# A mixture-of-experts layer whose down projection keeps tokens still and streams w_down

## What is computed

```
xf     = rmsnorm(x, g)                       # 1024 tokens x 1024
logits = xf @ w_router + b_router            # 32 experts
top_logits, top_idx = top_k(logits, 4)       # 4 experts a token
top_w  = softmax(top_logits)
for expert e, on the tokens that chose it:
    gu     = xb @ w_gate_up[e] + b_gate_up[e]          # 1024 -> 2048
    gate   = min(gu[:, 0::2], 7)
    up     = clip(gu[:, 1::2], -7, 7)
    hidden = (up + 1) * gate * sigmoid(1.702 * gate)   # 1024
    y      = hidden @ w_down[e] + b_down[e]            # 1024 -> 1024
x = x + sum over a token's experts of top_w * y
```

## Time and profile before

| | us |
|---|---|
| median of three executions | 2376.84 |
| profiled execution | 2372.35 |
| its span | 2370.5 |
| TensorE busy (matmul) | 2273.3 |
| VectorE busy | 941.1 |
| ScalarE busy | 460.3 |
| GpSimd busy | 225.1 |

### The profile page before, as it was taken

The page is one execution under the profiler, slowest core; times in us unless marked ns, Lnnn a source line. Parts: engine busy times, 40 slices in busy tenths (PEclk is TensorE's granted clock), DMA queues, the critical chain, the costliest instruction groups (busy, mean ns, idle before and its releaser), DMA issues.

```text
span 2370.5 us, 43566 instructions
## 1 busy us (share of the span) xinstructions
PE 2273.3 (96%) x17841; PEld 2164.4 (91%) x17842; DVE 941.1 (40%) x2192; ACT 460.3 (19%) x848; POOL 225.1 (9%) x172
## 2 busy tenths in 40 slices
PE   6999999999969999999999999999999999999997
PEld 5878888777869999999999999999999999999997
DVE  6434434875363333233333333433333332333332
ACT  4243143664101111111111111111111111111110
POOL 1101101100000100001010001100010110001001
PEclk9999999999979999999999999999999999999998
DMA  4222222105378887788888877886888886888882
GB/s 163 98 71 72 89 89 65 62 2 186 114 234 265 270 284 237 236 272 268 288 277 288 278 239 248 274 278 220 289 271 283 271 265 216 286 290 272 287 271 36
DMA packets 250615, 504.05 MB, mean 213 GB/s; under 512 B 7994, under 2 KB 36718, under 8 KB 250238
## 3 DMA queue, kind: packets, MB, share of 16 engines
q1 hardware_dynamic: 234268, 451.96, 54.9%
q0 software_dynamic: 14912, 45.71, 9.7%
q10 hardware_dynamic: 1344, 5.01, 0.7%
HBM read 469.46 MB, written 31.10 MB: 211 GB/s over the span
## 4 chain that ended last, share of the span: by engine, by line
PE 91%; DVE 4%; issue 3%; DMA 1%; ACT 0%; POOL 0%; DVEq 0%; ACTq 0%; SPq 0%; POOLq 0%
PE bank L1053 43%; PE bank L1064 19%; PE bank L804 12%; PE bank L1041 3%; DVE hx L1413 2%; PE bank L1012 2%; PE bank L921 2%; PE bank L908 2%; PE bank L956 1%; PE bank L958 1%; PE bank L957 1%; PE bank L1004 1%; PE bank L886 1%; PE bank L812 1%; PE bank L898 0%
## 5 line engine op out<-in xcount | busy, mean ns | idle before, releaser
L1053 PE MATMUL bank<-hx,ring 128*128 128x140 f32 (+1 forms) x8192 | 1037.6, 288 | 26.2 <-issue 16.7
L1053 PEld LDWEIGHTS bank<-hx,ring 128*128 128x128 f32 x8192 | 1021.4, 197 | 33.2 <-issue 32.2
L1064 PE MATMUL bank<-hx,ring 128*128 128x140 f32 (+1 forms) x4096 | 514.7, 287 | 0.0
L1064 PEld LDWEIGHTS bank<-hx,ring 128*128 128x128 f32 x4096 | 507.0, 190 | 0.0
L760 ACT ACTIVATE hx<-hx 128x168 f32<-128x168 f32 x256 | 87.9, 343 | 1447.0 <-DVE hx L1484 1447.0
L1484 DVE TENSOR_SCALAR hx<-bank,hx 128x168 f32<-128x168 f32 x256 | 100.4, 392 | 639.4 <-PE bank L1053 638.9
L1509 DVE TENSOR_SCALAR hx<-bank,hx 128x168 f32<-128x168 f32 x256 | 100.5, 392 | 353.8 <-PE bank L1064 353.8
L573 POOL DMA_INDIRECT out_x<-mix,hx x66 | 99.8, 1513 | 825.4 <-ACT mix L753 780.9
L552 POOL DMA_INDIRECT mix<-xn_scratch,hx x66 | 64.7, 981 | 718.8 <-DVE hx L1408 708.7
L804 PE MATMUL bank<-hx_r,mix_r 128*128 128x512 f32 x480 | 116.1, 401 | 7.9 <-DVE hx_r L1147 7.9
L804 PEld LDWEIGHTS bank<-hx_r,mix_r 128*128 128x128 f32 x480 | 92.1, 193 | 28.4 <-issue 9.2
(11 more groups left out here) (202 smaller groups left out, 1697.8 us busy)
## 6 DMA issues: line engine op xcount, KB each, us to landing
ring<-in_w_gate_up SPq DMA_DIRECT2D x128, 2048.0 KB, 10.8
ring<-in_w_down SPq DMA_DIRECT2D x64, 2048.0 KB, 8.8
mix<-in_w_in SPq DMA_DIRECT2D x14, 1024.0 KB, 5.0
work<-in_w_in SPq DMA_DIRECT2D x14, 1024.0 KB, 5.0
ring<-in_x SPq DMA_DIRECT2D x8, 512.0 KB, 8.2
hx<-in_w_out SPq DMA_DIRECT2D x1, 4096.0 KB, 14.1
work<-in_x ACTq DMA_DIRECT2D x8, 512.0 KB, 4.8
out_x<-work SPq DMA_DIRECT2D x8, 512.0 KB, 4.4
```

The source lines that it names most:

```text
L1053: mm = e.matmul(bank[f % 2][:, part * CAP:part * CAP + w], gu_ring[:, k, f * 256 + part:(f + 1) * 256:2], xT[:, k, 0:w], start=k == 0, sto ...
L1064: return e.matmul(bank[2 + j % 2][:, 0:w], dn_ring[:, k, j * P:(j + 1) * P], hid[:, k, 0:w], start=k == 0, stop=k == KD - 1)
```

## The change

The down projection is turned round. `hid` is now the stationary operand and w_down streams as moving operand, 512 columns a matmul, so that the result has tokens on partitions, and no transposes back are needed. As a stationary operand has at most 128 columns, one matmul series serves the first 128 tokens (`down_main`, banks 2 and 3, two halves t of the output by eight k). Tokens past 128 go in rounds r of 32 (`down_over`): the stationary operand is 32 tokens wide, and each quarter j of the output columns (256) goes to its own group of 32 array columns and PSUM partitions of bank 7. A round is done only where the block has more than 128 (or 160) tokens, by a branch on the count. CAP becomes 192, the widths 140, 168 and 192.

The bias b_down, which was added per partition, is now put into PSUM first, by bf16 matmuls with a stationary selector `sel` of the expert (a three-way split of b_down's float32 rows into bf16 sums; it is made once before the loop, on ScalarE and VectorE).

The token list has three columns of 128 slots: the first 128 tokens and, for each round, 32 tokens four times over, once for each output quarter. Gathers and adds are three indirect DMAs each: one of 128 rows of 4 KB and two of 128 quarter rows of 1 KB. `y_m` and `y_o`, which hold the scaled result, lie over the gathered rows `xg`, `xg_o`; ScalarE writes them at the end of the block itself (`weigh_rows`) after the next block's tokens have been turned, and GpSimd issues the next gather before the block's own adds. Token transposes are 8 + 4 of 128 x 128. w_down is loaded again only after the block's last down matmul (both halves wait for m_dn at n*2+2).

```diff
-CAP = 168
+OV = 32
+GR = P // OV
+RO = 2
+CAP = P + RO * OV
+NH = 1 + RO
-WIDTHS = (140, CAP)
+WIDTHS = (140, 168, CAP)
...
                 for c in range(2):
-                    e.wait_ge(m_dn, n * 8 + (4 * c - 4))
+                    e.wait_ge(m_dn, n * 2 + 2)
...
             def gather():
-                for h in range(2):
-                    e.indirect_dma_start(out=xg[:, h], out_offset=None, in_=xn_dram,
-                                         in_offset=bass.IndirectOffsetOnAxis(ap=idx[:, h:h + 1], axis=0)).then_inc(g_in, 16)
+                e.indirect_dma_start(out=xg, out_offset=None, in_=xn_dram,
+                                     in_offset=bass.IndirectOffsetOnAxis(ap=idx[:, 0:1], axis=0)).then_inc(g_in, 16)
+                for r in range(RO):
+                    e.indirect_dma_start(out=xg_o[:, r], out_offset=None, in_=xn_quarters,
+                                         in_offset=bass.IndirectOffsetOnAxis(ap=idx[:, 1 + r:2 + r], axis=0)).then_inc(g_in, 16)
...
             def block_dmas(n):
-                add_rows(n)
                 e.wait_ge(l_ok, n + 2)
-                e.wait_ge(g_tr, n * 3 + 3)
+                e.wait_ge(sc_done, n * 48 + 48)
                 e.sem_inc(pool_go, 1)
                 gather()
+                add_rows(n)
...
             def weigh_rows(n):
-                e.wait_ge(sc_done, n * 32 + 16)
-                for h in range(2):
-                    for q in range(2):
-                        m = 2 * h + q
-                        e.wait_ge(m_ytr, n * 4 + (m + 1))
-                        e.activation(yo[:, h, q * 512:(q + 1) * 512], bank[4 + m][0:HC, :], ACT.Copy,
-                                     scale=w_sc[:, h:h + 1]).then_inc(m_yo, 1)
+                e.wait_ge(l_keep, n + 1)
+                e.wait_ge(g_tr, n * 4 + 8)
+                for t in range(2):
+                    e.wait_ge(m_dn, n * 2 + (t + 3))
+                    e.activation(y_m[:, t * CH:(t + 1) * CH], bank[2 + t][:, :], ACT.Copy, scale=w_sc[:, 0:1]).then_inc(m_yo, 1)
+                for r in range(RO):
+                    e.activation(y_o[:, r], bank[7][:, r * 2 * P:(r + 1) * 2 * P], ACT.Copy,
+                                 scale=w_sc[:, 1 + r:2 + r]).then_inc(m_yo, 1)
...
             def turn_tokens():
-                for k in range(KD):
-                    for h in range(2):
-                        at = (k % 3) * CAP + h * HC
-                        mm = e.transpose(bank[4 + k // 3][:, at:at + HC], xg[:, h, k * P:(k + 1) * P],
-                                         cst[0:HC, C_ID:C_ID + HC])
-                    if k in (2, 5, 7):
-                        mm.then_inc(g_tr, 1)
+                for m in range(2):
+                    for q in range(4):
+                        mm = e.transpose(bank[4 + m][:, q * P:(q + 1) * P], xg[:, (4 * m + q) * P:(4 * m + q + 1) * P], ident)
+                    mm.then_inc(g_tr, 1)
+                for r in range(RO):
+                    for c in range(2):
+                        mm = e.transpose(bank[6][:, (2 * r + c) * P:(2 * r + c + 1) * P], xg_o[:, r, c * P:(c + 1) * P], ident)
+                    mm.then_inc(g_tr, 1)
...
+            def down_bias(t):
+                e.matmul(bank[2 + t][:, :], sel, bias_d[:, t * CH:(t + 1) * CH], start=True, stop=False,
+                         skip_group_check=True)
+            def over_bias():
+                for r in range(RO):
+                    for j in range(GR):
+                        e.matmul(bank[7][quarter_rows(j), r * 2 * P:(r + 1) * 2 * P], sel[:, 0:OV],
+                                 bias_d[:, j * 2 * P:(j + 1) * 2 * P], start=r == 0, stop=False, skip_group_check=True)
+            def down_main(n, t, k):
+                if t == 0:
+                    e.wait_ge(m_hid, n * 8 + (k + 3))
+                if k == 0:
+                    e.wait_ge(dn_in[t], n * 16 + 16)
+                mm = e.matmul(bank[2 + t][:, :], hid[:, k, 0:P], dn_ring[:, k, t * CH:(t + 1) * CH], start=False,
+                              stop=k == KD - 1, skip_group_check=True)
+                if k == KD - 1:
+                    mm.then_inc(m_dn, 1)
+            def down_over(r):
+                for k in range(KD):
+                    for j in range(GR):
+                        e.matmul(bank[7][quarter_rows(j), r * 2 * P:(r + 1) * 2 * P],
+                                 hid[:, k, P + r * OV:P + (r + 1) * OV], dn_ring[:, k, j * 2 * P:(j + 1) * 2 * P],
+                                 start=False, stop=k == KD - 1, skip_group_check=True)
...
                     mm.then_inc(m_gu, 1)
-                    if f == 0:
-                        turn_rows(n)
                     if f == 5:
...
+                e.wait_ge(s_sel, n + 1)
+                down_bias(0)
+                for k in range(KD):
+                    down_main(n, 0, k)
+                down_bias(1)
+                for k in range(4):
+                    down_main(n, 1, k)
+                e.wait_ge(g_in, n * 48 + 96)
+                turn_tokens()
+                for k in range(4, KD - 1):
+                    down_main(n, 1, k)
+                e.wait_ge(l_ok, n + 2)
+                over_bias()
+                with e.If(tokens > P):
+                    down_over(0)
+                if w > P + OV:
+                    with e.If(tokens > P + OV):
+                        down_over(1)
+                down_main(n, 1, KD - 1)
```

More of the change, by code:

```diff
@@ L62 @@
 GALPHA = 1.702
-C_ID, C_MB, C_BO, C_LS, C_ON, C_CA = (P * i for i in range(6))
+C_ID, C_ON, C_MB, C_BO, C_LS, C_CA = (P * i for i in range(6))
 C_IO = 6 * P
-C_I32 = C_IO + CAP
+C_I32 = C_IO + NH * P
 C_TID = C_I32 + NE
@@ L88, in constants @@
     t[:, C_CA:C_CA + P] = r <= c
-    t[:, C_IO:C_IO + CAP] = np.arange(CAP)
+    t[:, C_IO:C_IO + NH * P] = np.concatenate([np.arange(P)] + [P + OV * j + np.arange(P) % OV for j in range(RO)])
+    t[:, C_SEL:C_SEL + NE + 1] = r % NE == np.arange(NE + 1)[None, :]
+    t[:, C_J] = np.arange(P) // OV
     t[:, C_I32:C_I32 + NE] = np.arange(NE)
@@ L558, in _ @@
             e.wait_ge(e_st[1], 128)
-            e.dma_start(b_rows[:, 2048:3072], b_down[0]).then_inc(sc_done, 16)
+            for g in range(3):
+                e.dma_start(b_raw[g * NE:(g + 1) * NE], b_down[0]).then_inc(sc_done, 16)
             e.wait_ge(l_ok, 1)
@@ L769, in _ @@
                     block_act(n)
-            weigh_rows(more + NE)
         @block.tensor
@@ L1001, in token_list @@
             def token_list():
-                for h in range(2):
+                for h in range(NH):
                     for i in range(NT):
-                        mm = e.matmul(bank[7][0:HC, 5 * h:5 * h + 5], hot[:, i, h * HC:(h + 1) * HC], tw_s[:, i, :],
+                        mm = e.matmul(bank[7][:, 5 * h:5 * h + 5], hot[:, i, h * P:(h + 1) * P], tw_s[:, i, :],
                                       start=i == 0, stop=i == NT - 1)
@@ L1020, in _ @@
             e.wait_ge(bias_in, 16)
-            e.wait_ge(sc_done, 16)
             e.wait_ge(e_x2, 16)
-            for j in range(24):
-                if j < 16:
-                    src = b_rows[:, (j % 8) * 256 + j // 8:(j % 8) * 256 + 256:2]
-                else:
-                    src = b_rows[:, 2048 + (j - 16) * P:2048 + (j - 15) * P]
-                mm = e.transpose(bank[j // 12][:, (j % 12) * NE:(j % 12 + 1) * NE], src, cst[0:NE, C_ID:C_ID + NE])
+            for j in range(16):
+                mm = e.transpose(bank[j // 8][:, (j % 8) * NE:(j % 8 + 1) * NE],
+                                 b_rows[:, (j % 8) * 256 + j // 8:(j % 8) * 256 + 256:2], cst[0:NE, C_ID:C_ID + NE])
@@ L1047, in block_matmuls @@
+            def block_matmuls(n, w, tokens):
+                e.wait_ge(g_xT, n * 4 + 4)
                 for f in range(KD):
@@ L1113, in _ @@
                     block_pe(n)
-            turn_rows(more + NE)
         @block.vector
@@ L1444, in _ @@
             e.wait_ge(bias_ok, 3)
-            for m in range(3):
-                e.wait_ge(g_tr, m + 1)
+            for g in range(1, 3):
+                e.wait_ge(b_cast, g)
+                rows = slice(0, 3 * NE) if g == 1 else slice(2 * NE, 3 * NE)
+                e.tensor_tensor(b_raw[rows], b_raw[rows], bias_d[rows], ALU.subtract).then_inc(b_sub, 1)
+            for m in range(4):
+                e.wait_ge(g_tr, m + 1 if m < 2 else 4)
                 tokens_out(m)
-            for s_ in (m_up, m_gs, m_hid):
+            for s_ in (m_up, m_gs, m_hid, m_dn):
                 e.sem_inc(s_, 2)
+            e.sem_inc(m_yo, 4)
             grid = [P, NX, NE]
@@ L1505, in block_dve @@
                         list_out(n + 1)
-                e.wait_ge(m_ytr, n * 4 + 4)
-                for j in range(KD):
-                    e.wait_ge(m_dn, n * 8 + (j + 1))
-                    e.tensor_scalar(yT[:, j, :], bank[2 + j % 2][:, 0:CAP], be[:, 16 + j:17 + j], None, ALU.add)\
-                        .then_inc(m_y, 1)
-                    if j == 6:
```

(6 more changed lines are left out.)

204 lines of the change are left out of this document (96 added, 108 removed).

## The result

Slower. Four executions after the change took 2391.02 to 2396.31 us, median 2393.39, against 2375.59 (2370.44 to 2377.72) of the kernel before on the same chip: ratio 1.0081, 95% interval 1.0064 to 1.0098. The forecast was 2365, faster. That 2393 lies inside the stated range of 2350 to 2432 is luck: the range reached so far up mostly for rivals 1 and 3, slow column groups and late gathers, and neither came. The profiled execution spans 2390.0 us against 2370.5, at a mean granted clock of 0.973 against 0.981.

The account below looks back on a forecast made before the run. The loop was taken as a TensorE sum of streamed columns. Loop -19, fetch +4, gathers +2, before the loop +4.5, end -3 gave -11.5 us: about 2365 against the median 2376.84, range 2350 to 2432.

Parts of the forecast that it names:

- rival 1: Extra-token rounds: only two column groups run at a time, +65 us, 2430 (singly 2560); chance 0.20.
- Rival 3: Token gathers come late, so TensorE stands 1.5 us a block before the token transposes: +46 us, 2411; chance 0.13.
- Instruction fetch: Expert loop: longer code makes wide blocks jump further; +4 us taken, bounds -10 to +15.
- Rival 4: Expert loop: two fetch stalls in every wide block and one in some others, +25 us, 2390; chance 0.07.
- all that a block gains together: Each block's new down matmuls, bias, token list, token transposes and shape changes: 17.0 us, times 32 blocks 544.
- A round: Pass over 32 extra tokens, all four column groups at once: 3.65 us, 19 passes 69 us, bounds 69 to 265.
- rival 2: Extra-token rounds: four column groups run at a third of the time, not a quarter; +17 us, 2382; chance 0.10.
- w_down's late load: Load waits for the whole down stage: 4 MB takes some 11 us, wanted 31 us later, so hidden.
- VectorE's longer work: One-hot from 1.55 to about 3.4 us a block, evictions 25 ns longer each; nothing on the path.
- Ahead of the loop: Before the first block: longer one-hot, third gather and fourth eviction; +4.5 us taken, bounds 0 to +8.
- at the end: After the last matmul: three scalings and three scatters, some 15.4 us against 18.4; -3 taken, bounds -6 and +1.
- the gathers: Three gathers a block land just before the token transposes, cover under 1 us; 2 us in all, bounds 0 to 3 a block.

Follow-up runs that it names:

- e2: The kernel before with a third, never entered copy of TensorE's block code (width 168 again); 2414.34 us, ratio 1.018.
- experiment 2: Down stage written once behind the width choice (e3 2689.32 us, e4 2317.25); its count keeps eight 16-KB code pieces, drops the oldest, reads one ahead.
- e4: The changed kernel with widths 140 and 168 only and the down stage written once behind the width choice; 2317.25 us, ratio 0.9765.
- e8: e4 with a round's output quarters taken two at a time, 0 and 1 alternating over all k, then 2 and 3; 2367.56 us, ratio 0.9975.
- e6: e4 with a round's output quarters taken one by one, all eight k of each before the next; 2465.66 us, ratio 1.039.
- e13: e1 with its loop moved by 60 instructions (already met waits put ahead of it); 2324.6 us, ratio 0.9803.
- e14: The kernel before with its loop moved by 52 instructions (already met waits put ahead of it); 2360.3 us, ratio 0.9951.
- e3: The changed kernel, three widths kept, with the down stage written once behind the width choice instead of in each body; 2689.32 us, ratio 1.1359.
- e1: The changed kernel with two widths of TensorE's block code (140, 168) instead of three; 2341.82 us, ratio 0.9873.
- e12: e1 with its loop moved by 22 instructions (already met waits put ahead of it); 2348.6 us, ratio 0.9913.
- e10: e1 with its loop moved by 44 instructions (already met waits put ahead of it); 2361.1 us, ratio 0.9948.
- Experiment 4: Already met waits put ahead of TensorE's loop to move its code, in e1 (e10, e12, e13) and the kernel before (e11, e14); 2324.6 to 2390.6 us.
- e11: The kernel before with its loop moved by 36 instructions (already met waits put ahead of it); 2390.6 us, ratio 1.0071.
- e9: e4 plus 513 never executed instructions at the end of the block, inside the loop; 2817.3 us, ratio 1.1866.

## Why the prediction was wrong

**The step that failed** is the term "Instruction fetch": bounds -10 to +15 us, +4 taken. Measured: +49.3 us of "issue", and part of the clock behind it (mean 0.973 against 0.981, at most 19 us over the span, the stalls' own time among it). Rival 4 had the mechanism, at +25 and a chance of 0.07; it was too small as well. That its 2390 lies near the measured 2393 is luck: the stalls were twice as long, and the rest of the sum came out lower. Two parts of its reasoning failed:
- "TensorE's sequencer, though, will be ahead by longer matmuls." It isn't: the first late branch starts 2.50 us before the last matmul ends (951.71 and 954.21), and before the change it was 2.61 (944.42 and 947.03). The records of TensorE's sequencer at the end of the block before 971.29 show the jump over the third body at 3.84 us, the loop's branch back at 7.61 and the one to the wide body at 6.58. With what lies between and behind them that is 19.6 us, of which the lead hides 2.5. Before, one branch back of 3.35 us left 2.20 to be seen.
- The price was set by the stalls in the earlier trace rows, as if a second jump were one more of them. But two or three branches in a row then find their code gone, and behind the first, 3.3 to 3.8 us, the branch back of the loop takes 6.2 to 7.8 us, in the kernel after and in e2 alike. By the count of experiment 2, a wide block drops, from the eight pieces, those that the narrow blocks use, and the block behind fetches them again. The packets in the block behind are in the trace; which pieces they are is argued from the count, not seen.

The Trainium skill, page "Runtime: NRT & Kernel Launch", Instruction fetch mechanics, tells that a taken branch out of the fetched window stalls, and by it the prediction put up to 3 us more on a wide block. The runs agree that it stalls, and show 8 to 15 us more. They differ from the window of two pages that the section speaks of: e4 keeps six pieces over 32 passes. The same section also gives TensorE 128 KiB, filled first in, first out in blocks of 16 KiB; that would be eight pieces, and the count of experiment 2 agrees with it.

**What held,** each against its forecast:
- Blocks 47.2, 50.7 and 56.8 us (47.8, 51.4, 57.5). The records of 512 columns are 429 ns apart (432), the bias matmul 0.22 us (0.24), the token list 0.61 (0.75), the token transposes 1.31 (1.45), all that a block gains together 16.6 us (17.0).
- A round is 3.46 to 3.55 us (3.65), 64 records at 54 ns, four starting within 10 ns. Rivals 1 and 2 are out. e8 and e6 show what the first would have been: by twos 6.15 us a round (6.8 to 7.2 forecast), singly 11.3 (13.9); both are less because of the overlap where the quarter changes.
- Rival 3 is out: three gather issues of 0.95 to 1.00 us each, with 128 rows as with 84, not 1.35. GpSimd in the block shown:
```profile
1125.19 1.00 POOL L567 DMA_INDIRECT hx<-xn_scratch,small  x1 [23.07 <-DVE small L1442]
1126.49 0.97 POOL L570 DMA_INDIRECT hx<-xn_scratch,small  x1 [0.30 <-issue]
1127.77 0.95 POOL L570 DMA_INDIRECT hx<-xn_scratch,small  x1 [0.30 <-issue]
```
  The one place where TensorE waits for a gather is ahead of the first block. In the block that starts at 843.27 the third landed near 883.1, 2.1 us before the transposes; the 2 us put down for it were not needed.
- w_down's late load and VectorE's longer work: nothing, as said.
- Ahead of the loop +3.0 us (+4.5), at the end 16.8 against 18.4 us, -1.6 (-3).

Without the fetch term the forecast was -15.5 us, and e13 against e14 is -36. The rest is many terms each a little too large: 0.4 us a block x 32 = 13, 0.17 a round x 19 = 3, the gathers 2, ahead of the loop 1.5; what is left is within the noise of the runs.

**What stays open.** That the oldest piece goes, and where the pieces' borders lie, rests on a count that comes within five packets in nine of the twelve kernels, gives 55 to 63 for the 63 of the kernel after, and falls short by 10 in e2 and by 27 in e3; nothing in a trace shows it directly. It doesn't give the size of a stall: e1, e12 and e10 have nearly equal packets (46, 44, 44) and stand 19, 23 and 35 us. Experiment 4 shows part of the reason for e10; why the second of two such branches takes twice the first is not shown.

## What to carry to other kernels

Before code is added to a hardware loop, also code that no pass will run, count the engine's instructions in the loop and read the packets of the instruction queue: where they grow with the passes, some of the fetches make TensorE stand, mostly at a taken branch: here pieces of 2 to 17 us, seven of them on the 63 packets of the kernel after and seven on the 46 of e1, and the clock falls behind the long ones. Look first for a part that can be shared behind the branch (e4 against e1: the loop from 6.9 to 6.0 pieces, -25 us), and if that isn't possible try the same loop moved by some tens of instructions, which can also make it slower (e10, e11). Column groups pay in full if their matmuls alternate one by one in program order, and lose up to two thirds if they don't.

## What the runs showed of the hardware

- Four column groups of 32 with float32 operands: 64 records of 256 columns in 3.46 us, 54 ns each against 213 by the slope of the earlier trace rows, 3.9 times. The Trainium skill's 2.38x for three column tiles and 3.07x for four row tiles ("TensorE: Matmul & The Clock Gate", Part 3) are lower.
- Overlap of column groups reaches some four records in program order (e6, where the quarter changes); one by one, by twos and in turn the same records take 57, 97 and 179 ns.
- A loop of 6.0 pieces of 16 KB of code is kept on TensorE across 32 passes (e4: 8 packets after 675 us), and, well placed, one of 6.9 (e13, e14: 11); at eight pieces nearly all of it is fetched again in each pass (e9: 315 packets, e3: 285).
- The number of instructions ahead of a loop moved the time by +19 us (e10 on e1) and -17 (e13 on e1), with no work changed.
- The issue of a gather of 128 rows takes 0.96 us in the median if its rows are 1 KB and 1.00 if they are 4 KB.
